# Suffix sums of a stick-breaking attention: two float32r passes in place of fp32 matmuls, in a two-layer trunk on one core

## The reference, cut to what matters

```python
mask = s_idx < t_idx
log_1m = jnp.where(mask, jax.nn.log_sigmoid(-z), 0.0)
suffix = lax.cumsum(log_1m, axis=3, reverse=True) - log_1m
A = jnp.where(mask, jnp.exp(jax.nn.log_sigmoid(z) + suffix), 0.0)
out = A @ v
```

## Time and profile before

| what | value |
|---|---|
| median of three runs | 1793.2 us |
| lowest and highest | 1791.28 and 1795.0 us |
| time of the profiled execution | 1793.82 us |
| its span, first to last instruction | 1792.1 us |
| PE busy | 1571.5 us (88%) |
| DVE busy | 733.0 us (41%) |
| ACT busy | 421.0 us (23%) |
| POOL busy | 57.6 us (3%) |

### The profile page before, as it was taken

One profiled execution on the slowest core, in us unless ns is written; L12 is line 12 of the kernel. 1 busy time (PEld: TensorE's weight loads), 2 busy tenths in 40 slices (PEclk: granted clock), 3 DMA queues, 4 the chain that ended last, 5 costly groups with the idle time before them and its releaser, 6 DMA issues.

```text
span 1792.1 us, 25442 instructions
## 1 busy us (share of the span) xinstructions
PE 1571.5 (88%) x9809; PEld 1068.5 (60%) x9809; DVE 733.0 (41%) x1154; ACT 421.0 (23%) x559; POOL 57.6 (3%) x82
## 2 busy tenths in 40 slices
PE   7999999998977788778789999999988977888775
PEld 7999999886433234323287988988853442344322
DVE  4544444443422222222264756757343322232223
ACT  5344343432000000000154334334320000000002
POOL 4010000100000000000011000000000000000000
PEclk9999999998998998899799999999989888988896
DMA  8545454458999999999944465465679999999996
GB/s 266 192 145 182 148 182 164 144 211 310 381 424 425 427 425 425 425 427 424 409 167 141 144 208 170 158 207 169 234 313 426 423 425 426 427 425 424 425 426 265
DMA packets 149418, 543.77 MB, mean 303 GB/s; under 512 B 8736, under 2 KB 25456, under 8 KB 116208
## 3 DMA queue, kind: packets, MB, share of 16 engines
q1 hardware_dynamic: 148448, 541.14, 77.7%
q0 software_dynamic: 912, 1.82, 0.4%
HBM read 540.83 MB, written 2.10 MB: 303 GB/s over the span
## 4 chain that ended last, share of the span: by engine, by line
PE 51%; issue 27%; DMA 14%; SPq 3%; DVE 2%; ACT 1%; DVEq 0%; POOLq 0%; POOL 0%; ACTq 0%
PE psum_G L662 28%; PE psum_S L662 15%; DMA ring<-in_moe_w 14%; PE psum_A L662 4%; PE psum_T L662 3%; SPq L507 3%; DVE w_lo L406 1%; ACT w_hi L402 1%; DMA x<-in_x 0%; PE psum_A L669 0%; DVE x L1581 0%; ACT squares L1122 0%; POOLq L598 0%; DVE h L1816 0%; PE psum_T L881 0%
## 5 line engine op out<-in xcount | busy, mean ns | idle before, releaser
L662 PE MATMUL psum_A<-ring,arena 128*32 128x512 f32 x1984 | 301.8, 738 | 154.6 <-DMA ring<-in_moe_w 152.7
L406 DVE TENSOR_TENSOR w_lo<-ring,w_hi 128x2048 fp32r<-128x2048 f32 x126 | 289.2, 2298 | 289.0 <-ACT w_hi L402 284.8
L402 ACT CAST w_hi<-ring 128x2048 fp32r<-128x2048 f32 x128 | 244.1, 1908 | 244.4 <-PE psum_G L662 156.0
L662 PEld LDWEIGHTS psum_A<-ring,arena 128*32 128x32 f32 x1984 | 68.2, 121 | 332.9 <-issue 332.8
L1699 DVE COPY arena_two<-psum_A 128x512 f32<-128x512 f32 x64 | 44.3, 691 | 368.4 <-PE psum_A L662 368.0
L1729 DVE TENSOR_TENSOR x<-x,psum_S 128x512 f32<-128x512 f32 x128 | 87.9, 687 | 168.0 <-PE psum_S L662 168.0
L662 PE MATMUL psum_G<-xT_hi,w_hi 128*128 128x256 f32 x512 | 148.8, 291 | 2.1 <-DVE w_lo L406 1.8
L662 PE MATMUL psum_G<-xT_hi,w_lo 128*128 128x256 f32 x512 | 144.8, 283 | 0.0
L662 PE MATMUL psum_G<-xT_lo,w_hi 128*128 128x256 f32 x512 | 144.7, 283 | 0.0
L662 PE MATMUL psum_G<-ring,arena_two 128*32 128x512 f32 x1024 | 120.4, 612 | 17.3 <-DMA ring<-in_moe_w 17.2
L1278 ACT ACTIVATE arena<-psum_T 128x64 f32<-128x64 f32 x64 | 14.3, 224 | 507.5 <-PE psum_T L662 507.5
(11 more groups left out here) (224 smaller groups left out, 2098.9 us busy)
## 6 DMA issues: line engine op xcount, KB each, us to landing
ring<-in_moe_w SPq DMA_DIRECT2D x376, 1024.0 KB, 19.2
ring<-in_sb_w_in SPq DMA_DIRECT2D x48, 1024.0 KB, 5.0
ring<-in_ml_w_in SPq DMA_DIRECT2D x48, 1024.0 KB, 5.1
ring<-in_sb_w_out SPq DMA_DIRECT2D x16, 1024.0 KB, 4.9
ring<-in_ml_w_out SPq DMA_DIRECT2D x16, 1024.0 KB, 5.0
extra_one<-in_moe_w SPq DMA_DIRECT2D x4, 1024.0 KB, 8.1
extra_two<-in_moe_w SPq DMA_DIRECT2D x4, 1024.0 KB, 14.9
x<-in_x SPq DMA_DIRECT2D x2, 1024.0 KB, 6.6
```

Of the source, the lines that this page charges most:

```text
L402: act.copy(w_hi[:, slot_place(j), :], ring[:, slot_place(j), :]).then_inc(hi_made, 1)
L406: dve.tensor_tensor(w_lo[:, slot_place(j), :], ring[:, slot_place(j), :], w_hi[:, slot_place(j), :].bitcast(F32), ALU.subtract).then_inc(l ...
L662: return pe.matmul(dst, lhsT, rhs, start=start, stop=stop, skip_group_check=True)
```

## The change

A new step "round" of each head is put into `SB_STEPS` ahead of its "suffix" step. In it ACT waits for softplus_masked and copies `sp` into `sp_hi` as float32r (128x384), and DVE waits for that and writes `sp_lo` = `sp` - `sp_hi`, also float32r. PE's "suffix" step waits for the new semaphore softplus_lo and runs its three matmuls twice, over `sp_hi` and over `sp_lo`, all in float32r. The triangular and the full matrix of -1 become float32r tiles. In the merged list of a group the round steps stand at 10 and 13, and at 32 (behind the split and the chunk step of 32) and 37; in the output projection's list they stand at 7, 9, 24 (behind the split of 24) and 27.

```diff
--- before.py
+++ after.py
@@ -71,8 +71,8 @@
 
 
 
-SB_STEPS = [(2, "score", 0), (6, "score", 1), (14, "suffix", 0), (18, "suffix", 1),
-            (20, "score", 2), (26, "out", 0), (28, "score", 3), (30, "out", 1),
+SB_STEPS = [(2, "score", 0), (6, "score", 1), (10, "round", 0), (13, "round", 1), (14, "suffix", 0), (18, "suffix", 1),
+            (20, "score", 2), (26, "out", 0), (28, "score", 3), (30, "out", 1), (32, "round", 2), (37, "round", 3),
             (38, "suffix", 2), (42, "suffix", 3), (50, "out", 2), (54, "out", 3)]
 
 FIRST_STEPS = [(1 + n, "squares", n) for n in range(8)] + [(13, "rstd", 0), (27, "row", 0)]
@@ -157,8 +157,8 @@
 
         scales = sb("scales", [P, 5, KT])
         ident = sb("ident", [P, P])
-        neg_suffix = sb("neg_suffix", [P, P])
-        neg_ones = sb("neg_ones", [P, P])
+        neg_suffix = sb("neg_suffix", [P, P], F32R)
+        neg_ones = sb("neg_ones", [P, P], F32R)
         before = sb("before", [P, P])
         ones = sb("ones", [P, P])
         fold = sb("fold", [P, CAP])
@@ -203,6 +203,8 @@
         w_lo = at("w_lo", ring_at + 6 * 8 * KB, [P, HILO, SLOT], F32R)
         o_lo = at("o_lo", ring_at + 9 * 8 * KB, [P, KT, T], F32R)
         arena_three = at("arena_three", ring_at + 11 * 8 * KB, [P, 4096])
+        sp_hi = at("sp_hi", ring_at + 11 * 8 * KB + 9 * KB, [P, 2, TRI], F32R)
+        sp_lo = at("sp_lo", ring_at + 11 * 8 * KB + 12 * KB, [P, 2, TRI], F32R)
         arena = sb("arena", [P, ARENA])
 
         extra_slots = (at("extra_one", after_ring, [P, 2, SLOT]), at("extra_two", turned_at, [P, 2, SLOT]))
@@ -303,6 +305,8 @@
         softplus_log = sem("softplus_log")
         softplus_full = sem("softplus_full")
         softplus_masked = sem("softplus_masked")
+        softplus_hi = sem("softplus_hi")
+        softplus_lo = sem("softplus_lo")
         suffix_summed = sem("suffix_summed")
         prob_exp = sem("prob_exp")
         mask_begun = sem("mask_begun")
@@ -576,12 +580,12 @@
                                base=0, pattern=[[-1, P]], channel_multiplier=1)
             pool.drain().then_inc(ident_made, 1)
             pool.memset(fold[:, :], 0.0)
-            pool.memset(neg_ones[:, :], -1.0)
+            pool.memset(neg_ones[:, :].bitcast(F32), -1.0)
             pool.memset(ones[:, :], 1.0)
             pool.iota(iota[:, :], pattern=[[1, CAP]], base=1, channel_multiplier=0,
                       allow_small_or_imprecise_dtypes=True)
             pool.drain()
-            pool.affine_select(out=neg_suffix[:, :], in_=neg_ones[:, :], compare_op=ALU.is_ge, fill=0.0,
+            pool.affine_select(out=neg_suffix[:, :], in_=neg_ones[:, :].bitcast(F32), compare_op=ALU.is_ge, fill=0.0,
                                base=0, pattern=[[-1, P]], channel_multiplier=1)
             pool.affine_select(out=before[:, :], in_=ones[:, :], compare_op=ALU.is_gt, fill=0.0,
                                base=0, pattern=[[1, P]], channel_multiplier=-1)
@@ -839,11 +843,12 @@
                     mm(psum[a][:, 0:T], kT[:, k, 0:P], qT[:, k, :], True, False)
                     mm(psum[a][:, T:TRI], kT[:, k, P:T], qT[:, k, P:T], False, True).then_inc(filled[a], 1)
                 if step == "suffix":
-                    pe.wait_ge(softplus_masked, g * SBG + k + 1)
-                    s = sp[:, k % 2, :]
-                    mm(psum[a][:, 0:T], neg_suffix[:, :], s[:, 0:T], False, False)
-                    mm(psum[a][:, P:T], neg_ones[:, :], s[:, T:TRI], False, False)
-                    mm(psum[a][:, T:TRI], neg_suffix[:, :], s[:, T:TRI], False, True).then_inc(suffix_summed, 1)
+                    pe.wait_ge(softplus_lo, g * SBG + k + 1)
+                    for s in (sp_hi[:, k % 2, :], sp_lo[:, k % 2, :]):
+                        mm(psum[a][:, 0:T], neg_suffix[:, :], s[:, 0:T], False, False)
+                        mm(psum[a][:, P:T], neg_ones[:, :], s[:, T:TRI], False, False)
+                        last = mm(psum[a][:, T:TRI], neg_suffix[:, :], s[:, T:TRI], False, True)
+                    last.then_inc(suffix_summed, 1)
                 if step == "out":
                     if k == 0:
                         wait_chunk(0, g, 2)
@@ -1180,6 +1185,9 @@
                         act.activation(s, s, ACT.Exp)
                         act.drain()
                         act.activation(s, s, ACT.Ln, bias=1.0).then_inc(softplus_log, 1)
+                    if step == "round":
+                        act.wait_ge(softplus_masked, g * SBG + k + 1)
+                        act.copy(sp_hi[:, k % 2, :], sp[:, k % 2, :]).then_inc(softplus_hi, 1)
                     if step == "suffix":
                         act.wait_ge(suffix_summed, g * SBG + k + 1)
                         act.activation(prob[:, k % 2, :], psum[a][:, 0:TRI], ACT.Exp).then_inc(emptied[a], 1)
@@ -1458,6 +1466,10 @@
                         dve.wait_ge(softplus_log, g * SBG + k + 1)
                         dve.tensor_tensor(sp[:, k % 2, :], soft[:, k % 2, :], psum[a][:, 0:TRI], ALU.max)
                         dve.drain().then_inc(softplus_full, 1)
+                    if step == "round":
+                        dve.wait_ge(softplus_hi, g * SBG + k + 1)
+                        dve.tensor_tensor(sp_lo[:, k % 2, :], sp[:, k % 2, :], sp_hi[:, k % 2, :].bitcast(F32),
+                                          ALU.subtract).then_inc(softplus_lo, 1)
                     if step == "out":
                         dve.wait_ge(out_hi_made, g * SBG + k + 1)
                         at_ = bass.ds(g * SBG + k, 1)
```

## The result

The changed kernel takes 1814.05 us (median of four, 1810.89 to 1814.5), the kernel before 1793.01 us, measured beside it. The ratio is 1.0111, 95% interval 1.0099 to 1.0123: slower by 21 us, where 12 were forecast. The profiled execution has a span of 1812.6 us.

What follows compares the result with a forecast made beforehand. The prediction took PE to bound the mixing stage: 15.6 us of waits less 3.5 us of spared matmuls make 12.1 us more, on the median 1793.2 a forecast of 1805.3 us, range 1801 to 1814.

Steps and rivals of the forecast that it cites:

- PE is the bound of the stage: Mixing stage: PE busy for all 64 us of the stretch, so each microsecond it is spared or waits counts fully.
- The suffix matmuls: Suffix step of each head: 0.66 us in place of 0.88, sparing 3.5 us over 16 heads.
- the router's 0.106: Price in us taken for a narrow float32r matmul, from the router's 16 matmul records with 36 columns.
- The rival at the fp32 price: Narrow float32r matmuls in the suffix steps cost as much as fp32: 19.4 us more, 1812.6; chance 0.36.
- The waits: PE waits for DVE's subtraction at nine suffix steps: 11.4 us in three groups, 4.3 in the output projection, 15.6 together.
- the clock falls in the waits: Rival: each of the nine waits brings some 6 us at half clock, 3 us lost, 27 on top, 1832; chance 0.04.
- Absorbed waits: Rival: the 15.6 us come off the waiting for expert weights, 1789.7; chance 0.08 shared with rounds ahead of the splits.
- rounds ahead of the splits: Rival: DVE's rounds run before its splits, leaving one wait of 0.53 us, 1790.2; chance 0.08 shared with absorbed waits.
- The sign: Whole kernel: slower by more than the 3.6 us a measurement can tell; faster and same had 0.04 each.
- the likeliest number: Whole kernel: 1805.3 us, 12.1 more than the median before.

Runs made afterwards that it cites:

- e4: Against the kernel before: no round steps, PE runs six float32r matmuls twice over the rounded part and waits for the mask only; 1790.01 us, ratio 0.9982.
- e2: The change with unneeded fp32 matmuls (8 in a group's first and third suffix step; 2, 5, 10 in the output projection) ahead of PE's wait; 1804.62 us.
- e7: The change with a single unneeded fp32 matmul of 128 columns ahead of PE's wait in the suffix steps of heads 0 and 2; 1805.01 us.
- e3: The change with both roundings and the wait kept, but the three old fp32 matmuls over sp in place of the six float32r ones; 1808.74 us.
- e1: The change with its round steps in the groups' list at 7, 10, 31 and 37 in place of 10, 13, 32 and 37; 1790.32 us.
- e6: The change with the old fp32 matmuls in the suffix steps of heads 1 and 3, float32r ones in those of heads 0 and 2; 1813.76 us.
- e8: The change with only the round step of head 2 moved from 32 to 31, ahead of the split and the chunk step; 1800.27 us.
- e5: The change with the old fp32 matmuls in the suffix steps of heads 0 and 2, float32r ones in those of heads 1 and 3; 1807.17 us.

## Why the prediction was right or wrong

- *PE is the bound of the stage.* Right. Every wait of PE in it moved the end, and nothing of them came back later: the stage grew by 21.2 us and the whole span by 20.5, and the waits for expert weights are 158.6 us where they were 152.7.
- *The suffix matmuls.* Right, by more than the row deserved. I took 0.66 us a step from the router's 0.106; the first step above (0.73 less 0.10 for the late start, and 0.06 more for the matmul behind it) and e4 (0.88 - 0.19) both say 0.69. That the router's row, of fp32 matmuls of 36 columns, came so near is luck. The price isn't even, though: a narrow matmul takes 0.06 and the next one 0.11, and the wide one between them 0.17. The rival at the fp32 price, at 0.36, was wrong, though its 1812.6 is nearest to the result; e4 shows 3.1 us gained where it had 3.8 lost. The Trainium skill's 81 ns for a narrow matmul (TensorE: Matmul & The Clock Gate, Back-to-back issue gap) would have made it 0.56 us, 0.13 too little; the narrow ones are near it on the average of their two distances (0.085), and it is the wide one among them that costs more.
- *The waits.* Right, and in their places: nine, 15.5 us against 15.6; the first of a group 1.85 against 1.85. The second one of the output projection is shorter (0.94 by the profile's count, 1.2 in all, against 1.34).
- *The clock.* This is the step that failed: "the clock falls in the waits" had a chance of 0.04, and the waits, "0.5 to 2.4 us between long stretches of work", were taken for harmless, on the ground of one row, a single wait of 1.77 us after which PE ran at full pace (the starts go on from the earlier trace rows at 17.80 and 17.93). Six of seven waits of at least 1.59 us had a fall behind them. Its price was oversized where it was named, 3 us in each of nine waits; measured are 1.5 in six, 8.8 us, which is all of the difference between the forecast and the result. e2 and e7 show it: with work put into the waits, and the suffix steps starting no earlier, the falls are gone and so are 9 us. One harmless wait says little of the next: in e3, with other work behind them, six of the seven long waits were harmless and one was not. The Trainium skill (TensorE: Matmul & The Clock Gate, A second HAM failure mode: psum-queue depth-cycling) says that the clock swings where PE idles shortly between groups of matmuls frequently enough. Of that the trace agrees with the outcome, a change worse than its waits by 8.8 us. It doesn't agree with the condition: the long waits are 22 us and more apart, and each fall stands alone behind one of them.
- *Absorbed waits, rounds ahead of the splits.* Neither is what happened; the latter, as a kernel, is e1, forecast with one wait of 0.53 at 1790.2 and measured at 1790.32.
- *The forecast as a whole.* The sign was right, and the result, 1814.05, lies at the upper edge of the range (1801 to 1814); the likeliest number was 9 us low. That the range reaches so far is luck: its upper edge was made of the fp32 price of the narrow matmuls and of spread between executions, neither of which is in the result, and the falls of the clock, which are, had been put at 1832.

## What to carry to other kernels

Where engines take their steps from a list in program order, price an added step by what stands ahead of it in the list of each engine that does it, at the moment when the bound engine asks; total idle time says nothing. A wait of one or two microseconds on TensorE may cost twice: look for the stretch behind it whose matmuls are 0.21 us apart where they were 0.12, and suspect it all the more when the work right behind the wait is made shorter, as here. When the gain of a change is missing, move its steps in the order before giving it up: here the same work is 21 us slower or 3 us faster, and 5 with two of its matmuls merged.

## What the runs showed of the hardware that was not expected

- Float32r matmuls of 128 columns have no high price: 0.06 to 0.11 us to the next start, against 0.22 for fp32. At half the granted clock the same six matmuls took 1.15 us (364.94 to 366.09) in place of 0.73 with a late start.
- Idle times of 1.59 to 2.11 us in an otherwise full stream made the granted clock fall to 1.2 GHz for 3.4 us in six of seven cases; in e6 it was five of seven (1.58 to 2.12 us), in e8 two of three. With 0.22 us of other work in each such wait none did (e7); with the 0.2 us longer fp32 step right behind them, none (e5) or one of seven (e3), and that one began with PE's restart. What the chip weighs in this, and why like waits were spared, stays open.
